# Sliding attention scores for two heads at once, in two steps, alternating between the row halves of the array

## The reference

```python
for layer in range(2):
    shift, scale, gate = split(silu(c) @ ada_w[layer] + ada_b[layer])
    h = rms_norm(x, norm_w[layer]) * (1 + scale) + shift
    y = even_mixer(h) if layer == 0 else odd_mixer(h)
    x = x + gate * y
return rms_norm(x, final_norm_w)
```

```python
q, k, v, z = split(h @ w_in)
for each block n of 128 queries: keys = blocks n-1 and n (256 keys)
s = q @ k.T * 64**-0.5                   # 128 x 256
s = where(0 <= dist < 128, s - slope[head] * dist, -inf)
m = max(max(s), sink[head])
p = exp(s - m); p = p / (sum(p) + exp(sink[head] - m))
o = p @ v;   y = (o * silu(z)) @ w_out
```

## Time and profile before

| | us |
|---|---|
| median of 3 runs | 2177.07 (2175.12 to 2178.8) |
| the profiled execution | 2172.86 |
| its span, first to last instruction | 2171.1 |
| TensorE busy | 2066.2 (95%) |
| VectorE busy | 1123.1 (52%) |
| ScalarE busy | 752.4 (35%) |
| mean granted TensorE clock | 0.982 |

### The profile page before, as it was taken

The page is one execution under the profiler, slowest core; times in us unless marked ns, Lnnn a source line. Parts: engine busy times, 40 slices in busy tenths (PEclk is TensorE's granted clock), DMA queues, the critical chain, the costliest instruction groups (busy, mean ns, idle before and its releaser), DMA issues.

```text
span 2171.1 us, 28163 instructions
## 1 busy us (share of the span) xinstructions
PE 2066.2 (95%) x11503; PEld 1561.0 (72%) x11503; DVE 1123.1 (52%) x2030; ACT 752.4 (35%) x1547; POOL 0.2 (0%) x4
## 2 busy tenths in 40 slices
PE   6889999999999999999999799899999999998996
PEld 3247777777777777777776587687777777776875
DVE  1247575765757666575766322345454554463232
ACT  2443242432424233242333322344333433343221
POOL 0000000000000000000000000000000000000000
PEclk8999999999999999999999999999999999999998
DMA  8874433343343334334341334421122121213232
GB/s 299 334 309 156 134 128 127 126 140 122 118 145 117 129 124 145 118 126 144 119 135 50 100 128 140 146 93 59 59 83 78 63 78 64 78 39 120 103 105 99
DMA packets 59763, 270.43 MB, mean 125 GB/s; under 512 B 7410, under 2 KB 7796, under 8 KB 41588
## 3 DMA queue, kind: packets, MB, share of 16 engines
q1 hardware_dynamic: 59636, 268.64, 35.8%
HBM read 255.51 MB, written 13.11 MB: 124 GB/s over the span
## 4 chain that ended last, share of the span: by engine, by line
PE 85%; DVE 6%; ACT 4%; DMA 3%; issue 2%; SPq 1%; DVEq 0%; ACTq 0%
PE psum L549 23%; PE psum L551 20%; PE psum L550 20%; PE psum L679 3%; PE psum L918 3%; DMA ada_p<-in_ada_first 1%; PE psum L590 1%; PE psum L946 1%; DVE ada_acc L1404 1%; PE psum L930 1%; PE psum L729 1%; PE psum L738 1%; PE psum L765 1%; DVE w_lo L1367 1%; PE psum L783 1%
## 5 line engine op out<-in xcount | busy, mean ns | idle before, releaser
L549 PE MATMUL psum<-mov_hi,w_hi 128*128 128x512 f32 x2128 | 891.0, 419 | 36.9 <-DVE mov_lo L1417 11.3
L551 PE MATMUL psum<-mov_hi,w_lo 128*128 128x512 f32 x2128 | 836.7, 393 | 0.0
L550 PE MATMUL psum<-mov_lo,w_hi 128*128 128x512 f32 x2128 | 834.7, 392 | 0.0
L549 PEld LDWEIGHTS psum<-mov_hi,w_hi 128*128 128x128 f32 x2128 | 401.6, 189 | 174.6 <-issue 76.3
L551 PEld LDWEIGHTS psum<-mov_hi,w_lo 128*128 128x128 f32 x2128 | 401.5, 189 | 90.0
L550 PEld LDWEIGHTS psum<-mov_lo,w_hi 128*128 128x128 f32 x2128 | 403.1, 189 | 80.1 <-issue 8.6
L1367 DVE TENSOR_TENSOR w_lo<-w_raw,w_hi 128x512 fp32r<-128x512 f32 x532 | 353.7, 686 | 183.1 <-ACT w_hi L1032 181.6
L1032 ACT ACTIVATE w_hi<-w_raw 128x512 fp32r<-128x512 f32 x532 | 310.2, 619 | 6.7 <-DMA w_raw<-in_w_pack 6.7
L1404 DVE SCALAR_TENSOR_TENSOR ada_acc<-ada_t,silu_c,ada_acc 128x512 f32<-128x512 f32 x240 | 177.8, 741 | 1.8 <-DMA ada_t<-in_ada_late 0.9
L1727 DVE SCALAR_TENSOR_TENSOR res<-psum,mod,xr 128x512 f32<-128x512 f32 x32 | 24.0, 750 | 206.0 <-PE psum L551 204.7
L1257 ACT ACTIVATE osq<-res 128x512 f32<-128x512 f32 x32 | 20.2, 632 | 260.3 <-DVE res L1727 260.3
(11 more groups left out here) (272 smaller groups left out, 1795.4 us busy)
## 6 DMA issues: line engine op xcount, KB each, us to landing
w_raw<-in_w_pack SPq DMA_DIRECT2D x133, 1024.0 KB, 5.6
ada_t<-in_ada_late SPq DMA_DIRECT2D x128, 512.0 KB, 3.5
x_in<-in_ada_first SPq DMA_DIRECT2D x32, 512.0 KB, 7.0
ada_t<-in_ada_first SPq DMA_DIRECT2D x16, 512.0 KB, 8.6
ada_p<-in_ada_first SPq DMA_DIRECT2D x16, 512.0 KB, 9.0
xr<-x_spill SPq DMA_DIRECT2D x32, 256.0 KB, 2.7
x_in<-in_x SPq DMA_DIRECT2D x4, 1024.0 KB, 6.2
x_spill<-res SPq DMA_DIRECT2D x1, 4096.0 KB, 18.3
```

Source lines behind the costliest of these rows:

```text
L549: mm(PJ[r], w_hi[r][:, ks], mov_hi[:, kt], start=(j == 0), stop=False)
L550: mm(PJ[r], w_hi[r][:, ks], mov_lo[:, kt], start=False, stop=False)
L551: ins = mm(PJ[r], w_lo[r][:, ks], mov_hi[:, kt], start=False, stop=(j == KC - 1))
```

## The change

A step of scores now takes two heads of a pair (w) and two of the four query blocks (hf). It issues four products that alternate between the row halves, head 2w into SA0 and head 2w+1 into SA1. The two steps of a pair stand in slots 16w+8 and 16w+10, each waits until VectorE has taken the earlier results out of both banks. VectorE's operation over 128 x 1024 becomes four over 128 x 512 for a pair of heads; minima, exponentials and normalizations of the two heads follow each other, with a small tile `st1` for each head. Transposes move from 16w+14 and 16w+22 to 16w+16 and 16w+19, values and gating from 16w+23 to 16w+22. `gated1` waits for `z1_ok` too.

```diff
--- before.py
+++ after.py
@@ -175,7 +175,7 @@
         vall = sb("vall", [P, TT, 256], where=l1)
         kv_f = sb("kv_f", [P, T], where=l1)
         vcur = sb("vcur", [P, TT, 64], where=l1)
-        st1 = sb("st1", [P, 32], where=l1)
+        st1 = [sb(f"st1{i}", [P, 17], where=l1) for i in range(2)]
         u1 = sb("u1", [P, T], where=l1)
         between = ExitStack()
         xr = [sb(f"xr{i}", [P, T], where=between) for i in range(2)]
@@ -904,19 +904,19 @@
                     ins = nc.tensor.transpose(GO[:, i * P:i * P + P], kv_f[:, i * P:i * P + P], ident)
                 ins.then_inc(vup_ok, 1)
 
-            sc1 = lambda n: psum[:, 2 + n // 2, (n % 2) * 256:(n % 2) * 256 + 256]
             tr1 = lambda n: psum[:, 4 + n // 2, (n % 2) * 256:(n % 2) * 256 + 256]
 
-            def scores1(g, u):
-                if u == 0:
+            def scores1(g, w, hf):
+
+                if w == 0 and hf == 0:
                     pe.wait_ge(in_kv, g * 32 + 48)
-                if u % 2 == 0:
-                    pe.wait_ge(q1_ok, g * 4 + (u // 2 + 1))
-                if u > 0 or g > 0:
-                    pe.wait_ge(t1_ok, g * GH + u)
-                for n in range(4):
-                    ins = mm(sc1(n), q1[R[u % 2], (u // 2) * T + n * P:(u // 2) * T + n * P + P],
-                             kcur[R[u % 2], n * P:n * P + 256], start=True, stop=True)
+                if hf == 0:
+                    pe.wait_ge(q1_ok, g * 4 + w + 1)
+                wait(pe, t1_ok, 16 * g + 4 * w + 2 * hf)
+                for n in (2 * hf, 2 * hf + 1):
+                    for r in range(2):
+                        ins = mm((SA0, SA1)[r][:, n % 2 * 256:n % 2 * 256 + 256], q1[R[r], w * T + n * P:w * T + n * P + P],
+                                 kcur[R[r], n * P:n * P + 256], start=True, stop=True)
                 ins.then_inc(s1_ok, 1)
 
             def turn1(g, u):
@@ -951,11 +951,12 @@
             def group_stages(g):
 
                 st = {}
-                for u in range(GH):
-                    st.setdefault(8 * u + 8, []).append(lambda u=u: scores1(g, u))
-                    st.setdefault(8 * u + 14, []).append(lambda u=u: turn1(g, u))
                 for w in range(4):
-                    st.setdefault(16 * w + 23, []).append(lambda w=w: values1(g, w))
+                    st.setdefault(16 * w + 8, []).append(lambda w=w: scores1(g, w, 0))
+                    st.setdefault(16 * w + 10, []).append(lambda w=w: scores1(g, w, 1))
+                    st.setdefault(16 * w + 16, []).append(lambda w=w: turn1(g, 2 * w))
+                    st.setdefault(16 * w + 19, []).append(lambda w=w: turn1(g, 2 * w + 1))
+                    st.setdefault(16 * w + 22, []).append(lambda w=w: values1(g, w))
                 return st
 
             def group(g, before=None):
@@ -1297,8 +1298,8 @@
                 act.wait_ge(m1_ok, g * GH + u + 1)
                 for n in range(4):
                     f(pr[u % 2][:, n * 256:n * 256 + 256], pr[u % 2][:, n * 256:n * 256 + 256], ACT.Exp,
-                      scale=-1.0, bias=st1[:, n:n + 1], accum_out=st1[:, 4 + n:5 + n])
-                f(st1[:, 8:12], st1[:, 0:4], ACT.Exp, bias=st1[:, 16:17]).then_inc(p1_ok, 1)
+                      scale=-1.0, bias=st1[u % 2][:, n:n + 1], accum_out=st1[u % 2][:, 4 + n:5 + n])
+                f(st1[u % 2][:, 8:12], st1[u % 2][:, 0:4], ACT.Exp, bias=st1[u % 2][:, 16:17]).then_inc(p1_ok, 1)
 
             def turn1_copy(g, u):
                 act.wait_ge(tr1_ok, g * GH + u + 1)
@@ -1309,9 +1310,11 @@
 
             def group_stages(g):
                 st = {}
-                for u in range(GH):
-                    st.setdefault(8 * u + 9, []).append(lambda u=u: exps1(g, u))
-                    st.setdefault(8 * u + 14, []).append(lambda u=u: turn1_copy(g, u))
+                for w in range(4):
+                    st.setdefault(16 * w + 11, []).append(lambda w=w: exps1(g, 2 * w))
+                    st.setdefault(16 * w + 13, []).append(lambda w=w: exps1(g, 2 * w + 1))
+                    st.setdefault(16 * w + 16, []).append(lambda w=w: turn1_copy(g, 2 * w))
+                    st.setdefault(16 * w + 19, []).append(lambda w=w: turn1_copy(g, 2 * w + 1))
                 return st
 
             def group(g, before=None):
@@ -1760,29 +1763,36 @@
                 V.scalar_tensor_tensor(out=res[:, bass.ds(g * (4 * T) + c * T, T)], in0=u1[:], scalar=1.0,
                                        in1=PJ[w_ring(N_L1 + 2 * c + 1)], op0=ALU.add, op1=ALU.mult).then_inc(z1_ok, 1)
 
-            def biased1(g, u):
-                blk = lambda ap: ap.rearrange("p (n c) -> p n c", n=4)
-                dve.wait_ge(s1_ok, g * GH + u + 1)
-                if u >= 2 or g > 0:
-                    dve.wait_ge(tr1_ok, g * GH + (u - 1))
-                V.scalar_tensor_tensor(out=pr[u % 2][:], in0=dist1[:], scalar=con("slope1")[:, bass.ds(g * GH + u, 1)],
-                                       in1=psum[:, 2:4, :].rearrange("p a c -> p (a c)"), op0=ALU.mult, op1=ALU.subtract)\
-                    .then_inc(t1_ok, 1)
-                dve.wait_ge(t1_ok, g * GH + u + 1)
-                step(V.tensor_reduce(st1[:, 0:4], blk(pr[u % 2][:]), AX, ALU.min))
-                V.tensor_copy(st1[:, 16:17], sink[:, bass.ds(g * GH + u, 1)])
-                V.tensor_scalar(st1[:, 0:4], st1[:, 0:4], nsink[:, bass.ds(g * GH + u, 1)], None, ALU.min).then_inc(m1_ok, 1)
+            blk = lambda ap: ap.rearrange("p (n c) -> p n c", n=4)
+
+            def biased1(g, w, hf):
+
+                dve.wait_ge(s1_ok, 8 * g + 2 * w + hf + 1)
+                if hf == 0:
+                    wait(dve, tr1_ok, GH * g + 2 * w)
+                for r in range(2):
+                    V.scalar_tensor_tensor(out=pr[r][:, hf * 512:hf * 512 + 512], in0=dist1[:, hf * 512:hf * 512 + 512],
+                                           scalar=con("slope1")[:, g * GH + 2 * w + r:g * GH + 2 * w + r + 1],
+                                           in1=(SA0, SA1)[r], op0=ALU.mult, op1=ALU.subtract).then_inc(t1_ok, 1)
+
+            def maxima1(g, w, r):
+                u, s_ = g * GH + 2 * w + r, st1[r]
+                dve.wait_ge(t1_ok, 16 * g + 4 * w + 3 + r)
+                step(V.tensor_reduce(s_[:, 0:4], blk(pr[r][:]), AX, ALU.min))
+                V.tensor_copy(s_[:, 16:17], sink[:, u:u + 1])
+                V.tensor_scalar(s_[:, 0:4], s_[:, 0:4], nsink[:, u:u + 1], None, ALU.min).then_inc(m1_ok, 1)
 
             def normalize1(g, u):
-                blk = lambda ap: ap.rearrange("p (n c) -> p n c", n=4)
+                s_ = st1[u % 2]
                 dve.wait_ge(p1_ok, g * GH + u + 1)
-                step(V.tensor_tensor(st1[:, 4:8], st1[:, 4:8], st1[:, 8:12], ALU.add))
-                step(V.reciprocal(st1[:, 12:16], st1[:, 4:8]))
+                step(V.tensor_tensor(s_[:, 4:8], s_[:, 4:8], s_[:, 8:12], ALU.add))
+                step(V.reciprocal(s_[:, 12:16], s_[:, 4:8]))
                 V.tensor_tensor(blk(pr[u % 2][:]), blk(pr[u % 2][:]),
-                                st1[:, 12:16].unsqueeze(2).to_broadcast([P, 4, 256]), ALU.mult).then_inc(r1_ok, 1)
+                                s_[:, 12:16].unsqueeze(2).to_broadcast([P, 4, 256]), ALU.mult).then_inc(r1_ok, 1)
 
             def gated1(g, w):
                 dve.wait_ge(pv1_ok, g * 4 + w + 1)
+                dve.wait_ge(z1_ok, g * 4 + w + 1)
                 y = res[:, bass.ds(g * (4 * T) + w * T, T)]
                 V.scalar_tensor_tensor(out=y, in0=GO, scalar=0.5, in1=y, op0=ALU.mult, op1=ALU.mult).then_inc(y1_ok, 1)
 
@@ -1792,11 +1802,14 @@
 
             def group_stages(g):
                 st = {12: [lambda: v_group(g)]}
-                for u in range(GH):
-                    st.setdefault(8 * u + 8, []).append(lambda u=u: biased1(g, u))
-                    st.setdefault(8 * u + 11, []).append(lambda u=u: normalize1(g, u))
                 for w in range(4):
-                    st.setdefault(16 * w + 23, []).append(lambda w=w: gated1(g, w))
+                    st.setdefault(16 * w + 8, []).append(lambda w=w: biased1(g, w, 0))
+                    st.setdefault(16 * w + 10, []).append(lambda w=w: biased1(g, w, 1))
+                    st.setdefault(16 * w + 11, []).append(lambda w=w: maxima1(g, w, 0))
+                    st.setdefault(16 * w + 12, []).append(lambda w=w: maxima1(g, w, 1))
+                    st.setdefault(16 * w + 14, []).append(lambda w=w: normalize1(g, 2 * w))
+                    st.setdefault(16 * w + 15, []).append(lambda w=w: normalize1(g, 2 * w + 1))
+                    st.setdefault(16 * w + 22, []).append(lambda w=w: gated1(g, w))
                 return st
 
             def group(g, before=None):
```

## The result

| | before | after |
|---|---|---|
| median, us | 2176.4 (2175.12 to 2178.8, 4 runs) | 2144.01 (2142.59 to 2144.97, 4 runs) |
| ratio | | 0.9849, 95% interval 0.9832 to 0.9866 |
| profiled execution / its span, us | 2172.86 / 2171.1 | 2144.36 / 2142.3 |

Faster by 32.4 us by the medians, 28.5 by the two profiled executions; forecast were 30.3, and a median of 2146.8, from the three runs known then.

The account below looks back on a forecast made before the run. TensorE's queue was taken to bound the kernel; 27.5 us from the scores' steps plus 2.8 at the tail made 30.3, taking the median from 2177.07 to 2146.8 us. The forecast (78%) had its own range of 2143 to 2150.

Parts of the forecast that it names:

- A step: Scores on TensorE: four products hold the queue 1.06 us instead of 1.92, saving 0.86 us in each of 32 steps, 27.5 us.
- the sum for the second step: TensorE's schedule within a pair: the second step of scores starts 3.99 us after the first.
- the alternation: Order of a step's products: alternating between row halves puts four passes in line instead of eight, 1.06 us a step.
- The softmax chain: VectorE and ScalarE after the scores: first head normalized at 13.14 us, transposes at 13.35, 0.2 us to spare, no wait.
- the rival of the late transposes: First head's transposes late by 0.3 to 0.6 us, 5 to 10 us back, 2152 to 2157 us; chance 10%.
- The evacuation: VectorE taking scores out of PSUM: a 1.40 us pair against 2.9 us between the steps, so not the bottleneck.
- The overlap's factor: Scores step: the skill's 3.07 times for four tiles, scaled to 1.54 for two, would give 1.32 us and save 19 us.
- The tail: End of the last group: a shorter first stop and no fall of the clock together save 2.8 us.
- The first stop's 1.1 us: TensorE's stop for mov_lo at the end of the last group: 2.5 us in place of 3.63, saving 1.1.
- A stop of 2.34 us brought no fall of the clock, so I count the 1.7 us as gained: End of the last group: with a first stop of 2.5 us the clock would not fall, saving 1.7 us.
- the 1.00 around the tail's first stop: Sign of being right: a granted clock of 1.00 around TensorE's first stop at the end of the last group.
- What SP loads behind the gating follows as before: End of the last group: SP's loads after the last gating would follow as before; no gain or loss was counted.

Follow-up runs that it names:

- e2: Changed kernel with both products of a pair reading the upper row half, so no second half is used; 2170.67 us, ratio 0.9982 to the kernel before.
- e1: Changed kernel with a step's products ordered as both blocks of the first head, then both of the second; 2142.08 us, ratio 0.9848 to the kernel before.
- e5: Changed kernel with all eight products of a pair in one step (four banks), first head's eight passes queued before the second's; 2153.06 us, one run.
- e3: Changed kernel with the first head's transposes and their copy one slot earlier, at 16w+15; 2162.69 us, ratio 0.9943 to the kernel before.
- e7: Changed kernel with a pair's products in one step and minima, exponentials, normalizations, transposes, values and gating in earlier slots; 2131.18 us, ratio 0.98 to the kernel before.
- e8: e7 with ScalarE's mov_hi and VectorE's mov_lo ahead of each tail slot's attention stages, the first slot's ahead of the last z chunk; 2126.51 us, ratio 0.9777.

## Why the prediction was right, point by point

- **A step.** Forecast 1.06 us for four products in two halves, measured 1.06; saved per step 0.86, by the periods 1.70 a pair, 0.85 a step. L765 with its one pair in 0.63 us was the right row to build on, and e2 shows that the gain goes with the second half. The periods alone carry 16 x 1.70 = 27.2 of the 27.5 us. (In the sum for the second step, 3.99 should read 3.98; no term changes by more than 0.01.)
- **The reason given was too narrow.** The prediction took the alternation for the cause. e1 has none and is as fast. L765's rows held this already: its four passes are in the queue as two of one map and two of the other, and the changed kernel, too, has two passes of a head in a row, since a product is two passes. What is needed is that the free half's pass is at most three passes of the busy half behind (e5).
- **The softmax chain.** Forecast: normalization done at 13.14, transposes at 13.35, margin 0.2; measured 13.19, 13.41 and 0.22, and 2.59 for the first half's results against 2.6. e3 shows the margin is real. No stop came in any of the 16 pairs; the rival of the late transposes didn't occur.
- **The evacuation.** VectorE's pair took 1.41 us, and the second step came 1.46 us after it ended. The Trainium skill's warning in TensorEngine Tiling (Array Packing), section PSUM Bottleneck, which speaks of a fourfold speedup, was not borne out here, where a step is 1.8 times as fast.
- **The overlap's factor.** The estimate for two tiles, scaled down from the Trainium skill's figure for four in TensorE: Matmul & The Clock Gate, section Measured speedup vs the span model, would have made the step 1.32 us; it took 1.06. Past the fixed part of 0.2 us the two halves cost nothing to each other.
- **The tail: near in sum by luck, with two terms wrong.** Forecast 2.8 us, measured 5.7 less one pair's 1.7, 4.0. The first stop's 1.1 us was about right (1.27, from 3.63 to 2.36). The term "A stop of 2.34 us brought no fall of the clock, so I count the 1.7 us as gained" failed: in the profile after, the clock falls to half (1.2 GHz) behind stops of 2.36 and 2.25 us, 0.83 in both stretches of ten us above, so there were two falls in each profile and nothing was gained; the 1.00 around the tail's first stop, which the prediction named as a sign of being right, did not come. And "What SP loads behind the gating follows as before" failed: SP waits for the last gating before it loads the weights (code, L519), and they land 9.4 us behind its start before and 9.2 after. Before, the gating started at 1967.77 and TensorE went on with the weights at 1978.66, 10.9 us; after, at 1940.81 and 1951.58, 10.8 us. The gating now stands ahead of one more tail slot of 2.7 us, so the stop shrank from 4.49 to 1.94. These 2.55 us, and a stop of 0.40 for `osq` that went, came in place of the 1.7 of the clock; that the sum was near is luck.

## What to carry to other kernels

- Products with 64 rows cost half, past a fixed 0.2 us a step, when the ones in the free row half stand behind at most three passes of the busy half (e1, e5). In all runs here the two halves wrote different banks at a time; the same bank was not tried. Look for steps in which all lie in the same half, and join the steps of two heads.
- Before such a change lay out the chain of the other engines for the joined step, wait by wait, from rows of the old trace; here the margin was forecast at 0.2 us and measured at 0.22, and transposes one slot earlier cost 18.7 us.
- A load that waits for a result moves with that result and not with the engine that will want it: ask of each late stop which event it hangs on.

## What the runs showed of the hardware

- TensorE starts passes out of the order of its queue when they lie in the other row half: three passes (with their weight loads) of the busy half may stand ahead, not four (e1, e5). The Trainium skill, TensorE: Matmul & The Clock Gate, section The mechanism, has matmuls start in program order; in e5 the second head's first pass, ninth in the queue, starts at 0.973 us and the first head's sixth at 1.183, so the measurement decides against it.
- Two row halves streaming side by side for 16 passes cost each other nothing: 1.93 us for 16 passes, 1.92 for 8 in one half.
- The clock fell to half after stops of 2.36 and 2.25 us in the profile after, and did not after 2.34 in the one before, nor after 2.10 and 2.25 in e7's; in e3's it fell after 2.10 and not after 2.25. Within 60 us of the last pair's scores it fell twice, twice, once, once, once, once and twice in before, after and e1 to e5, and not at all in e7 and e8. The stops for mov_lo add up to 5.8 to 6.1 us in after, e1 to e5 and e7 alike, so a gain or loss of 1.7 us by the clock could not be forecast here from the length of stops of 2 to 2.5 us.
